# Reading the moving tile and writing the accumulator in descending order, with a 128-byte margin

## The reference

```python
# first block
h_l @ w_in, q_a @ w_q_b, kv_a @ w_kv_b, mix @ w_out
u = dwconv3(h @ w_up, cw, cb); (a * silu(g)) @ w_down          # 2048 x 11008, 5504 x 2048
# second block
z = hn @ w_in; a @ w_proj_a; bfx @ w_proj_b; merged @ w_out
jnp.square(jax.nn.relu(hm @ w_up)) @ w_down                    # 2048 x 8192, 8192 x 2048
```

## Time and profile before

| | |
|---|---|
| median of 3 runs | 2706.45 us (2701.42 to 2707.03) |
| the profiled execution, its own time | 2703.56 us |
| its span, first to last instruction | 2701.8 us |
| mean granted TensorE clock in it | 0.984 of full |
| PE (matmul) busy | 2606.8 us, 96% |
| DVE, ACT, POOL busy | 1758.9, 1222.5, 112.5 us |
| fetched from HBM | 548.53 MB, 204 GB/s over the span |

### The profile page before, as it was taken

One profiled execution on the slowest core, in us unless ns is written; L12 is line 12 of the kernel. 1 busy time (PEld: TensorE's weight loads), 2 busy tenths in 40 slices (PEclk: granted clock), 3 DMA queues, 4 the chain that ended last, 5 costly groups with the idle time before them and its releaser, 6 DMA issues.

```text
span 2701.8 us, 51009 instructions
## 1 busy us (share of the span) xinstructions
PE 2606.8 (96%) x21322; PEld 2522.5 (93%) x21322; DVE 1758.9 (65%) x2033; ACT 1222.5 (45%) x1487; POOL 112.5 (4%) x196
## 2 busy tenths in 40 slices
PE   6899988989999999999999999999999999999998
PEld 4699877889999999999999999999999999999997
DVE  5989776778888755665865655555665555555554
ACT  6753333345454544444544445444444444434433
POOL 0000323300000000000000110000000000000000
PEclk9899999989999999999999999999999999999999
DMA  9878766757777665565665555666566666666662
GB/s 353 283 227 271 254 210 206 240 174 242 250 242 250 208 198 173 168 220 175 197 189 155 180 159 160 194 194 193 192 183 195 193 195 194 189 194 195 194 210 95
DMA packets 289063, 553.55 MB, mean 205 GB/s; under 512 B 19386, under 2 KB 28712, under 8 KB 288232
## 3 DMA queue, kind: packets, MB, share of 16 engines
q1 hardware_dynamic: 288328, 548.53, 63.8%
q10 hardware_dynamic: 544, 2.29, 0.2%
HBM read 548.53 MB, written 2.10 MB: 204 GB/s over the span
## 4 chain that ended last, share of the span: by engine, by line
PE 84%; DVE 9%; ACT 3%; issue 2%; DMA 1%; POOL 1%; SPq 0%; ACTq 0%; DVEq 0%; POOLq 0%
PE half L1887 25%; PE half L1889 25%; PE half L1888 25%; DVE wlo L1100 4%; DMA raw<-in_w_ada 1%; ACT whi L618 1%; DVE acc L1129 1%; PE half L1921 1%; PE half L1923 1%; PE half L1922 1%; DVE acc L1132 1%; DVE tmp L1213 0%; PE half L2168 0%; PE half L2141 0%; PE half L2140 0%
## 5 line engine op out<-in xcount | busy, mean ns | idle before, releaser
L1100 DVE TENSOR_TENSOR wlo<-raw,whi 128x1024 fp32r<-128x1024 f32 (+1 forms) x909 | 1089.3, 1211 | 777.5 <-ACT whi L618 775.7
L618 ACT ACTIVATE whi<-raw 128x1024 fp32r<-128x1024 f32 (+1 forms) x909 | 940.5, 1048 | 1038.6 <-PE half L1889 922.6
L1887 PE MATMUL half<-hf,whi 128*128 128x256 f32 x2400 | 668.2, 278 | 6.4 <-DVE hf L1192 5.2
L1888 PE MATMUL half<-hf,whi 128*128 128x256 f32 x2400 | 666.2, 278 | 0.0
L1889 PE MATMUL half<-hf,wlo 128*128 128x256 f32 x2400 | 666.2, 278 | 0.0
L1887 PE MATMUL half<-hid,whi 128*128 128x256 f32 x1712 | 475.0, 277 | 1.2 <-DVE wlo L1100 1.2
L1888 PE MATMUL half<-hid,whi 128*128 128x256 f32 x1712 | 474.4, 277 | 0.0
L1889 PE MATMUL half<-hid,wlo 128*128 128x256 f32 x1712 | 474.4, 277 | 0.0
L1887 PEld LDWEIGHTS half<-hf,whi 128*128 128x128 f32 x2400 | 451.3, 188 | 8.5 <-issue 5.8
L1889 PEld LDWEIGHTS half<-hf,wlo 128*128 128x128 f32 x2400 | 453.0, 189 | 0.0
L1888 PEld LDWEIGHTS half<-hf,whi 128*128 128x128 f32 x2400 | 452.1, 188 | 0.0
(11 more groups left out here) (290 smaller groups left out, 3020.4 us busy)
## 6 DMA issues: line engine op xcount, KB each, us to landing
raw<-in_w_up SPq DMA_DIRECT2D x288, 512.0 KB, 4.3
raw<-in_w_in SPq DMA_DIRECT2D x216, 512.0 KB, 4.0
raw<-in_w_down SPq DMA_DIRECT2D x212, 512.0 KB, 4.5
raw<-in_w_ada SPq DMA_DIRECT2D x192, 512.0 KB, 5.2
raw<-in_w_out SPq DMA_DIRECT2D x64, 512.0 KB, 4.8
raw<-in_w_proj_a SPq DMA_DIRECT2D x16, 512.0 KB, 4.5
raw<-in_w_proj_b SPq DMA_DIRECT2D x16, 512.0 KB, 4.2
raw<-in_w_up SPq DMA_DIRECT2D x16, 384.0 KB, 3.4
```

Of the source, the lines that this page charges most:

```text
L618: A(whi[:, s, 0:elems], raw[:, c, 0:elems], ACT.Copy).then_inc(s_hi_ready, 1)
L1100: V.tensor_tensor(wlo[:, s, 0:elems], raw[:, c, 0:elems], whi[:, s, 0:elems].bitcast(F32), ALU.subtract).then_inc(s_drained, 1)
L1887: mm(o, hi, x[:, 0:T], start=(k == 0 and b % 2 == 0), stop=False, skip_group_check=True)
L1888: mm(o, hi, x[:, T:2 * T], start=False, stop=False, skip_group_check=True)
```

## The change

Line 298 gets a tile of 32 float32 (128 bytes in each partition) that nothing uses. It lies behind `square_sum` and ahead of the scopes of all activation tiles, so these move up by 128 bytes while `whi` and `wlo` stay; 192 bytes of distance become 320. And `block` hands TensorE the same operands with the step -1 in place of 1: the moving operand is read from its last column to its first, and the output piece is written from its last column to its first. Column j of the product still lands at column j. The weights are read as before. Products outside `block` keep their order, though those that read an activation tile read it at the new place. Nothing else moves: each engine has the same instructions in the same order with the same waits.

```diff
         square_sum = sb("square_sum", [P, TB, 4])
+        sb("margin", [P, 32])
...
             def block(o, b, hi, lo, x, k, nk):
 
-                mm(o, hi, x[:, 0:T], start=(k == 0 and b % 2 == 0), stop=False, skip_group_check=True)
-                mm(o, hi, x[:, T:2 * T], start=False, stop=False, skip_group_check=True)
-                return mm(o, lo, x[:, 0:T], start=False, stop=(k == nk - 1), skip_group_check=True)
+                o, xh, xl = o[:, ::-1], x[:, 0:T][:, ::-1], x[:, T:2 * T][:, ::-1]
+                mm(o, hi, xh, start=(k == 0 and b % 2 == 0), stop=False, skip_group_check=True)
+                mm(o, hi, xl, start=False, stop=False, skip_group_check=True)
+                return mm(o, lo, xh, start=False, stop=(k == nk - 1), skip_group_check=True)
```

## The result

The changed kernel takes 2793.99 us in the median of three runs (2793.32 to 2795.71), where the one before took 2706.45: a ratio of 1.033, estimated over all runs, 95% interval 1.0307 to 1.0354 (the medians alone give 1.0323), or +87.5 us. The forecast was -25 us with a range up to 2772. The profiled execution took 2795.71 us, its span is 2793.9.

A forecast was written before the change was run, and what follows sets the result against it. The prediction took TensorE's matmul pace in `block` as the bound. The descending read with the new distance gave -25 us, the other parts nothing: 2706.5 - 25 = 2681.5, say 2682 us, range 2610 to 2772.

The forecast's parts named there:

- The bound and the multiplier: TensorE, busy 96% of the span, bounds the kernel; any pace change in `block` counts 19,590 matmuls.
- The levels of before: In `block` before the change, matmuls start either 113.3 ns apart or 117.8 ns apart, at the same clock.
- The bad end: The descending read at the new distance puts all `block` matmuls at 117.8 ns: +63 us.
- the three ends: Outcomes for `block`'s descending read at the new distance: 107.8 ns (-133 us), 113.3 ns (-25 us) or 117.8 ns (+63 us).
- the middle: `block`'s matmuls keep 113.3 ns wherever the stream starts, against a mean of 114.6: -25 us, the outcome chosen.
- the lower level: The pace of 113.3 ns a matmul in `block`, taken to hold 70% of the time before the change.
- the three prices: Costs the earlier trace can't show: `block`'s descending read with the new distance, its descending write, and products outside `block`.
- its full price of +1934 us: `block`'s descending write goes one column in two cycles, 213.3 ns a matmul against 114.6.
- the last: `block`'s descending stream falls to 117.8 ns a matmul or a little above: +63 us, 2769 us; chance 0.17.
- The first: The loss on each `block` matmul shrinks below that at 113.3 ns: 2574 to 2670 us; chance 0.20.
- The second: The change doesn't matter; `block` keeps 113.3 and 117.8 ns, shared out anew: 2706 us, give or take 9; chance 0.22.
- Rival three: `block`'s descending PSUM writes go singly instead of in pairs: up to 1934 us slower, about 4640 us; chance 0.09.

The follow-up runs named there:

- The ascending sweep: Ascending order at distance 320; beyond the first slice each block loads 8 weight columns, starting 0 to 224 bytes into its weights; one execution took 2691.5 us.
- 8 columns at position 0 alone: The changed kernel, but beyond the first slice a block's weights are only their first 8 columns; step 120.0 ns, one execution 2794.26 us.

## Why the prediction was wrong

**What held.** The bound and the multiplier: the three lines hold the chain, 6530 groups before and after, and the step from start to start sets the time. The levels of before, the share of about 30% at the upper in its profiled execution (a count gives 28%; it is no constant, as the other kernels at 192 and 448 show), and that nothing but `block`'s pace would move. That the supply follows: ACT waits longer for TensorE, and DVE for ACT. The bad end's mechanism, a uniform level, came true, one step higher than I had put it.

**The step that failed** is the choice among the three ends: "Of the three ends I take the middle." I took the lower level for the likely one because it held 70% of the time. But that share was a property of the very distance and direction that the change gives up. The runs show that 113.3 ns stands at the distance 192 in ascending order alone, among six distances ascending and four descending; each other combination that was run has 117.7 to 120.1. The signs that I read as evidence against the distance all came from the one distance of before, as the text itself said of the three prices. A good state at the one point measured says that a change of that point is more likely to leave it than to improve it.

**The terms.** The read's bad end was set at +63 us, as if no level lay above 117.8, and steps above it had a chance of 0.03 beyond the range. Measured are 120.0 ns and +106 us before the smaller waits, +87.5 in all. The descending read brings a loss that stays, about 118 ns, even with 8-column loads at eight addresses, and with full loads the new distance brings it from 117.7 to 120.0. In ascending order the same new distance costs 50 us alone. Of the write I had its full price of +1934 us in the sum as an end: it is 0.

**The rivals.** Closest was the last, the stream falling into the upper level "or one a little above it", with +63 us and a chance of 0.17. The first (a smaller loss) didn't come true in any of the runs: none of the windows from 2050 to 2600 us shows less than 113.2 ns a matmul. The second rested in part on the earlier trace rows, in which 8-column weights keep the pace, and took from them that the distance may be idle. The ascending sweep shows why they couldn't tell: so short a load costs at one distance in eight only. The earlier trace rows show three matmuls that paid nothing. Rival three is excluded by its own run. I weighed the Trainium skill's PSUM rule at 0.09, and the run of the write alone shows it has no hold on a step of -1.

**What stays open.** Why the distance 192 has two levels, and what picks one when the stream restarts: the kernels at 192 and 448 have both, in different shares, and none was made to control it. Why the descending read loses at all, and why its step of 120.0 ns with 8 columns at position 0 alone falls to about 118 with loads spread over eight positions. How a load of 128 columns comes to its steps at 64 to 160 and at 224: that the two reads meet is argued from the short loads and shown nowhere directly. The descending order was run with full loads at four distances, so a good one between them isn't excluded, though the short loads lose at all eight positions.

## What to carry to other kernels

- Where two operands stream at once, treat the distance of their start addresses as a tuning parameter: here 32 to 64 bytes of padding cost or gave back 2 to 3% of the whole kernel, so any edit that moves a tile can bring such a difference along. Compare layouts at equal distance before you judge anything else.
- Read the pace from start to start (or from counts in a stretch), not from durations: for `hid`, a mean duration of 277 against 282 ns stood over a step of 113 against 120.
- If a kernel stands in its better state at the one point that its trace shows, a change of that point deserves a forecast with more weight on the loss.

## What the runs showed of the hardware

- With fp32r operands of 256 columns at the clock of 1.00, a matmul's mean step over 550 us was 113.3 ns at best and 120.1 at most in these runs, by the distance between the weights' and the moving operand's addresses modulo 256 bytes (64 and 320 alike, 192 and 448 alike) and by the direction of the moving read.
- Beside an ascending read, loads of 8 columns cost 5.5 ns at one distance of eight, once for the three loads there, and nothing at the others. Loads of 128 columns brought the step to 117.7 ns or more at every distance tried but 192, where 113.3 and 117.8 ns both occur; steady patterns such as 120, 115, 118 ns in turn stand beside single levels.
- The descending read of the moving operand costs 4 to 6 ns a matmul even with 8 columns of weights (117.5 to 119.5 ns against 113.4 ascending).
- Writing the accumulator in descending order is free (ratio 1.0003, 0.9989 to 1.0018).
